# Prompt attention of a streaming encoder step: the next tile's keys are turned at the second head, its queries at the fifth

## What is computed

```python
qa, ka, va, qb, kb, vb, qi, ki, wi = _mixer_inputs(yp, pos_p, mix_norm[l], w_in[l])
# group A (x = 0): each chunk of 64 queries sees its own chunk and the 8 before it
sc = einsum('bcqhd,bckhd->bchqk', chunked(q), k_band) * (d ** -0.5)
sc = where(valid, sc + bias, -inf)
o_a = einsum('bchqk,bckhd->bcqhd', softmax(sc), v_band)
# group B (x = 1): each query sees the 256 keys that an indexer selected
sc = einsum('bqhd,bqkhd->bqhk', q, kg) * (q.shape[-1] ** -0.5)
o_b = einsum('bqhk,bqkhd->bqhd', softmax(where(valid, sc, -inf)), vg)
yp = yp + concat([o_a, o_b], axis=-1) @ w_out[l]
```

## Time and profile before

| | |
|---|---|
| median of 3 runs | 2784.23 us (2777.97 to 2785.0) |
| the profiled execution | 2785.24 us |
| its span | 2783.6 us |
| TensorE matmul busy (PE) | 2608.2 us, 94% |
| TensorE weight loads busy (PEld) | 2332.9 us, 84% |
| VectorE (DVE) | 1355.5 us, 49% |
| ScalarE (ACT) | 986.1 us, 35% |
| GpSimd (POOL) | 512.9 us, 18% |
| mean granted TensorE clock | 0.973 |
| DMA | 294.28 MB, mean 106 GB/s |

### The profile page before, as it was taken

The page is one execution under the profiler, slowest core; times in us unless marked ns, Lnnn a source line. Parts: engine busy times, 40 slices in busy tenths (PEclk is TensorE's granted clock), DMA queues, the critical chain, the costliest instruction groups (busy, mean ns, idle before and its releaser), DMA issues. The chain is left out here.

```text
span 2783.6 us, 40367 instructions
## 1 busy us (share of the span) xinstructions
PE 2608.2 (94%) x16684; PEld 2332.9 (84%) x16684; DVE 1355.5 (49%) x2437; ACT 986.1 (35%) x1666; POOL 512.9 (18%) x368
## 2 busy tenths in 40 slices
PE   6999999999999999976998989989899999999997
PEld 6999999988878899974776766657799999998886
DVE  6523232335553698985777723323642323233544
ACT  5332323233432323133666532222433232323332
POOL 0233444100001122821000000000043334410000
PEclk9999999999999999988999989999999999999999
DMA  3122221366622121213000334542112222136553
GB/s 121 48 82 73 84 80 63 121 231 209 226 108 63 65 82 48 97 35 123 24 31 24 122 108 154 178 173 85 46 63 82 72 85 80 63 118 233 194 212 121
DMA packets 153109, 294.28 MB, mean 106 GB/s; under 512 B 14032, under 2 KB 90456, under 8 KB 152928
## 3 DMA queue, kind: packets, MB, share of 16 engines
q1 hardware_dynamic: 146688, 268.12, 28.3%
q0 software_dynamic: 6240, 23.59, 2.3%
HBM read 237.26 MB, written 61.78 MB: 107 GB/s over the span
## 5 line engine op out<-in xcount | busy, mean ns | idle before, releaser
L803 DVE TENSOR_TENSOR f_dl<-f_raw_d,f_dh 128x2048 fp32r<-128x2048 f32 x66 | 151.3, 2293 | 274.6 <-ACT f_dh L619 274.6
L619 ACT ACTIVATE f_dh<-f_raw_d 128x2048 fp32r<-128x2048 f32 x66 | 126.5, 1916 | 322.1 <-PE f_pV L151 292.2
L2082 PEld LDWEIGHTS t_po<-t_v,t_pT 128*128 128x128 f32 x1056 | 134.1, 193 | 34.7 <-DVE t_osb L1806 14.3
L569 ACT ACTIVATE f_gh<-f_pX 128x256 f32<-128x256 f32 x120 | 49.3, 411 | 319.5 <-PE f_pX L151 319.5
L1939 ACT ACTIVATE t_sc<-t_sc,t_small 128x640 f32<-128x640 f32 (+8 forms) x136 | 99.9, 735 | 162.9 <-DVE t_small L1867 128.5
L150 PE MATMUL f_pX<-f_xop,f_u_shi 128*128 128x256 f32 x504 | 149.2, 296 | 0.0
L151 PE MATMUL f_pX<-f_xop,f_u_slo 128*128 128x256 f32 x504 | 149.2, 296 | 0.0
L149 PE MATMUL f_pX<-f_xop,f_u_shi 128*128 128x256 f32 x504 | 149.2, 296 | 0.0
L149 PE MATMUL w_pw<-i_hi,r_T_hi 128*128 128x256 f32 (+1 forms) x504 | 145.2, 288 | 2.6 <-PEq L351 2.6
L150 PE MATMUL w_pw<-i_lo,r_T_hi 128*128 128x256 f32 (+1 forms) x504 | 145.5, 289 | 0.0
L151 PE MATMUL w_pw<-i_hi,r_T_lo 128*128 128x256 f32 (+1 forms) x504 | 144.8, 287 | 0.0
(11 more groups left out here) (372 smaller groups left out, 8138.3 us busy)
## 6 DMA issues: line engine op xcount, KB each, us to landing
f_raw_d<-in_ffn_w_down SPq DMA_DIRECT2D x66, 1024.0 KB, 5.0
hid<-f_gh SPq DMA_DIRECT2D x22, 1152.0 KB, 9.0
f_raw_h<-hid SPq DMA_DIRECT2D x66, 384.0 KB, 5.5
f_g_raw<-in_ffn_w_gate SPq DMA_DIRECT2D x21, 1024.0 KB, 5.3
f_u_raw<-in_ffn_w_up SPq DMA_DIRECT2D x21, 1024.0 KB, 6.4
proj<-w_stage POOLq DMA_DIRECT2D x12, 1152.0 KB, 5.6
i_raw<-in_w_in SPq DMA_DIRECT2D x12, 1024.0 KB, 5.1
f_x<-in_x_prompt SPq DMA_DIRECT2D x16, 512.0 KB, 6.8
```

Of the source, the lines that this page charges most:

```text
L569: act.activation(dst, by_tile(pX[:, c, 0:N[c]]), ACT.Copy).then_inc(s_copy, 1)
L619: act.activation(d_hi[slot(q)][:], raw_d[slot(q)][:], ACT.Copy).then_inc(s_dhi, 1)
L803: dve.tensor_tensor(d_lo[slot(q)][:], raw_d[slot(q)][:], d_hi[slot(q)][:].bitcast(F32), ALU.subtract)
L2082: last = pe.matmul(po[:, h * HD:(h + 1) * HD], pT[:, g % 2, j * P:(j + 1) * P], v[x][:, k0 + j, h * HD:(h + 1) * HD], start=j == 0, stop=j ...
```

## The change

The step **prep** becomes two, **keys** and **queries**. The queries of tile n + 1 stay at h = 4, ahead of the turn. The keys move to h = 1 of tile n, behind score g + 2 and ahead of value g - 1. The list `order`, which says in which order `pm` is filled, follows: keys of n + 1, output of n - 1, queries of n + 1, where it was output, keys, queries. On TensorE the wait for the loaded rows goes with the keys; on ScalarE the copy to `kT` stands behind the exponential of head h = 3. Tile 0 keeps keys and queries one behind the other. No instruction is added or removed, and the loads' waits are unchanged.

```diff
--- before.py
+++ after.py
@@ -1515,14 +1515,16 @@
 
     heads = [(x, t, h) for x in range(2) for t in range(NP) for h in range(H)]
     tiles = [(x, t) for x in range(2) for t in range(NP)]
-    plan = [("prep", 0, 0), ("score", 0), ("score", 1)]
+    plan = [("keys", 0, 0), ("queries", 0, 0), ("score", 0), ("score", 1)]
     for g, (x, t, h) in enumerate(heads):
         n = tiles.index((x, t))
         if h == 4 and n + 1 < len(tiles):
-            plan.append(("prep",) + tiles[n + 1])
+            plan.append(("queries",) + tiles[n + 1])
         plan.append(("turn", g))
         if g + 2 < len(heads):
             plan.append(("score", g + 2))
+        if h == 1 and n + 1 < len(tiles):
+            plan.append(("keys",) + tiles[n + 1])
         if g >= 1:
             plan.append(("value", g - 1))
         if h == 2 and n >= 1:
@@ -1662,8 +1664,8 @@
             lo_n[key] = nlo
         order = []
         for e in plan:
-            if e[0] == "prep":
-                order += [(("k",) + e[1:], 0), (("q",) + e[1:], 0)]
+            if e[0] in ("keys", "queries"):
+                order += [((e[0][0],) + e[1:], 0)]
             elif e[0] == "out":
                 order += [(("o",) + e[1:], 1)]
         order += [((("sk", "sq")[j], x), 0) for x in range(2) for j in range(2)]
@@ -1942,11 +1944,13 @@
         def _(act):
             act.wait_ge(s_zero, 1)
             for e in plan:
-                if e[0] == "prep":
+                if e[0] == "keys":
+                    x, t = e[1:]
+                    act.wait_ge(s_mf, misc[("k", x, t)] + 1)
+                    act.activation(kT[x][:, :, t * P:(t + 1) * P], pm[:].rearrange("p (f c) -> p f c", c=P), ACT.Copy).then_inc(s_ma, 1)
+                elif e[0] == "queries":
                     x, t = e[1:]
                     n = x * NP + t
-                    act.wait_ge(s_mf, misc[("k", x, t)] + 1)
-                    act.activation(kT[x][:, :, t * P:(t + 1) * P], pm[:].rearrange("p (f c) -> p f c", c=P), ACT.Copy).then_inc(s_ma, 1)
                     act.wait_ge(s_mf, misc[("q", x, t)] + 1)
                     if n >= 2:
                         act.wait_ge(s_s, (n - 1) * H)
@@ -2033,11 +2037,13 @@
         @block.tensor
         def _(pe):
             for e in plan:
-                if e[0] == "prep":
+                if e[0] == "keys":
+                    x, t = e[1:]
+                    pe.wait_ge(s_row, 32 * (x * NP + t + 1))
+                    pe_rows(pe, ("k", x, t), rows[:, 0, :])
+                elif e[0] == "queries":
                     x, t = e[1:]
                     n = x * NP + t
-                    pe.wait_ge(s_row, 32 * (n + 1))
-                    pe_rows(pe, ("k", x, t), rows[:, 0, :])
                     pe_rows(pe, ("q", x, t), rows[:, 1, :])
                     if n == 0:
                         pe.wait_ge(s_bias, 16)
```

## The result

The changed kernel took 2754.56 us (median of 4 runs, 2752.39 to 2757.85), beside 2784.61 us for the kernel before; the ratio is 0.9898, with a 95% interval of 0.988 to 0.9917. Later comparisons add runs. The kernel before took 2781.3 us in the median of 32 runs (2776.98 to 2787.7), the changed one 2754.6 in the median of 8 (2750.47 to 2760.82): 26.7 us.

A forecast was written before the change was run, and what follows sets the result against it. TensorE was taken to bound the prompt attention's long tiles. 25.9 us going, less 1.4 and 2.0 coming back, saved 22.5 from 2785.24: 2762.7, or 2761.7 from the median; forecast 2762.5, range 2757 to 2773.

The forecast's parts named there:

- The base of the sum: Whole kernel: the profiled execution before the change, 2785.24 us, from which the saving was subtracted.
- What bounds, and the stall: Prompt attention: TensorE bounds long tiles; its wait for copied keys, 16.7 us in 15 waits, is removable.
- What goes, 25.9: Between keys and queries, 15 preparations: 19.3 us of stall and 6.6 of key transposes leave.
- What comes back, 1.4: Second head: key transposes mostly fit the hole before the first head's value; 1.4 us return.
- Tile 0's 0.9: Tile 0's second head: the 0.44 us of key transposes cost about 0.9 at 1.2 GHz.
- the 0.7 of the next paragraph: Tile 0: the extra 0.58 us key copy on a nearly full ScalarE loses 0.7 us.
- ScalarE's side, 2.0: Tiles 0, 1, 5, 8 and 9: the moved key copy and later ScalarE work give back 2.0 us.
- Rival (a): Tile 0 and 1459 to 1472: TensorE's low clock goes too, returning 1 to 3 us; chance 0.08.
- (b): Prompt attention: ScalarE becomes the bound, saving only 10.8 us, 2774.4; chance 0.14 with mixtures.
- (c): Bank pm: the output waits as the queries did, saving 4.4 us, about 2780.8; chance 0.06 with late loads.
- (d): Tiles 0 to 3: TensorE's clock stays at 1.2 GHz, making the kernel slower, 2798; chance 0.04.
- Loads that come late: Keys wanted after five heads, tightest in tile 1: 1.1 us at the maximum landing; shared chance 0.06.

The follow-up runs named there:

- e2: Changed kernel with the keys turned behind the first head's value at the second head, not ahead of it: 2760.14 us.
- e3: Changed kernel with the keys turned at the fourth head instead of the second, one head ahead of the queries: 2780.57 us.
- e1: The kernel before, unedited, run and profiled once more: 2781.17 us.
- e5: Changed kernel with the keys ahead of the fifth head's turn and the queries behind the score that follows it: 2761.1 us.
- e9: The changed kernel, unedited, run again: ratio 0.9915 to the kernel before.
- e4: Changed kernel with one extra ScalarE copy of the turned keys ahead of the copy to kT: 2761.4 us.
- e6: Changed kernel with the queries turned at the sixth head instead of the fifth: 2758.0 us.
- e7: Changed kernel with the third head's turn issued ahead of the first head's value: 2755.22 us.
- e8: Changed kernel with queries at the sixth head and the third head's turn ahead of the first head's value: 2752.46 us.
- e11: Changed kernel with three extra chained ScalarE copies of the turned keys ahead of the copy to kT: 2770.97 us.

## Why the prediction was right and wrong

Two steps of the prediction failed, and either alone would have left the time inside the range. The base of the sum, 2785.24 us (the range allowed for 1.0 less), lies 3.9 above the median of 32 runs; what was put down as coming back, 1.4 + 2.0 = 3.4 us, measured 1.9 (1.4 in tile 0, 0.4, 0.6 and 0.2 in the spacings of tiles 5, 7 and 13, less 0.8 of small gains in the others), and the clock in tile 9, put at nothing in the sum, gave 1.3. (2781.3 less the 22.5 forecast is 2758.8, and 2784.23 less the 26.7 measured is 2757.5: both lie in the range.)

**What bounds, and the stall: right.** TensorE's wait for t_kT was a pure loss. With it out, a five-block tile is shorter by 1.69 us (1.6 forecast), heads stay 2.69 to 2.70 apart, and nothing behind the stretch changed its length.

**What goes, 25.9: right.** For the 14 preparations between the first and the last output the gaps from keys to queries sum to 24.0 us; the gain there was 24.8, of which 1.3 are the clock in tile 9. All 15 gaps sum to 25.9.

**What comes back, 1.4: too high.** The holes took the key transposes in all middle tiles (e2: 0.42 to 0.44 each when they can't). Tile 14 lost 0.26 of the 0.44 put down for it. Tile 0's 0.9 can be had only together with the 0.7 of the next paragraph. From its first turn to the first output it took 14.59 and 15.23 us in two profiles of before (14.59 in e3 as well), 14.11 and 14.12 in two of after. Its gap was 1.92, so 1.4 us were lost against the profiled run and 0.8 against e1, where the clock was down for longer; forecast were 1.6.

**ScalarE's side, 2.0: too high.** Two of its terms measured as forecast: tile 5 gained 1.84 of its 2.23 (0.3 forecast as lost, 0.39 lost), and tile 8's output got a wait, 0.49 marked, which cost 0.60 in the spacing (1.05 of 1.65). Tile 5's loss stands where it was forecast, at the sixth head:

```profile
1376.52 0.74 PE L2028 MATMUL t_pt<-r_ident,t_sc 128*128 128x128 f32 x5 [0.25 <-ACT t_pT L1977]
```

But tiles 1 and 8 gained 0.22 and 0.15 more than their gaps, where I had put losses of 0.2 each. In tiles 1 and 9 the loss is there, a new wait of a value for t_pT of 0.23 each; what covers it is the wait for T_lo at the fifth head, which fell from 1.02 to 0.57 in tile 1, from 1.29 to 1.00 in tile 8 and from 0.77 to 0.60 in tile 9. I had counted on that for tile 1 alone. And I left out a gain: queries that follow a value directly take 0.44 to the next turn, not the 0.49 they took behind a stall, 0.05 in each tile (24.66 to 22.97 is 1.69, and the gap was 1.65).

**Rival (a), 0.08: it came.** The low stretch of the clock in tile 9 is in all three profiles that have the spacings of the kernel before (before, e1, e3) and in neither of after. Before (two windows), then after at the same place in the program, over a longer window:

```profile
1469.00:1472.00 3.00, 2.39 (x10) 2.22 (x11) 0.01 (x1) 1.81 (x5) 0.00 (x0) 0.62 0.10 23
1472.00:1475.00 3.00, 3.00 (x20) 2.68 (x19) 2.34 (x9) 1.85 (x7) 0.00 (x0) 0.81 0.46 157
```

```profile
1440.00:1459.00 19.00, 16.52 (x108) 13.51 (x109) 15.73 (x48) 13.07 (x41) 0.00 (x0) 1.00 0.10 29
```

Tile 9 gained 2.83 us where the gap was 1.55: 1.3 us of clock, the term that (a) priced at 1.2. I should have given it more than a chance of 0.08. The likely cause is idle time of TensorE, which the change removes. The Trainium skill's rule ("TensorE: Matmul & The Clock Gate", part 1), weighed in the prediction, pointed that way; in this tile the trace agrees, with 0.62 before and 1.00 after. That the stall behind the keys is the cause is not shown: e2 and e5, where it is gone or small, have low stretches in tile 12, e2 also in tile 8. Between tile 0 and the last output six of the twelve profiles have none (after, e9, e4, e6, e7, e8, all with the keys in the hole at the second head) and six have at least one; e11, with the keys there and ScalarE held up, is one of these. But tile 12's wait of 1.52 us for t_osb is the same in before, at 1.00 behind it, as in e2 and e5. No run isolates idle time as the cause.

**The base: wrong, and the other half of the miss.** I counted from 2785.24 us. Only 3 of 32 runs of before took longer; their median is 2781.3. The three runs that I had spread over 7.0 us and their mean was 2782.4, so the range should have had more than 1.0 us for the base. So the miss of 7.9 us is 3.9 from the base and 4.2 from the saving (26.7 by medians over all runs, 25.3 by the mean of two profiles each, for the 22.5 forecast), less 0.2 of rounding. Of the 4.2, 1.5 are losses that were put too high (1.9 instead of 3.4), 1.3 are tile 9's clock, and 1.4, the difference between 26.7 and 25.3, are not seen in the stretch of any profile. The division goes by all runs; in the first comparison, of four runs each, the kernel before had 2784.61 and the saving was 30.0.

**The other rivals.** (b) is out by e4; of the waits for t_pT that would have shown it, long tiles have only tile 5's. (c) lives in one tile: the output of tile 8. (d) didn't come: 1297 to 1344 was at 1.00 throughout. Loads that come late were not seen either; no wait for t_rows is left but the first.

## What to carry to other kernels

When one engine walks a plan together with others, a step has a place in each engine's order, and what a wait costs is set by the two places together: moving the producer's part past work in which the copying engine has no share (e3) changes nothing. Fill a hole of the bounding engine with work that it must do anyway, and look for the hole with the named wait: here it paid 0.44 us a tile for the keys and 2.8 us more for a turn (e7). Count from the middle of many runs of the old kernel, not from the one that was profiled.

## What the runs showed of the hardware that I had not expected

The same code ahead of the stretch ended anywhere between 1262.4 and 1271.1 us in twelve profiles, with granted clocks of 0.98 and 1.00 in the same 100 us window. TensorE's clock fell in short tiles without any long stop: in e1 to 0.51 in a stretch of 3 us that follows one with TensorE busy 1.31 of 3.00 us at 1.00.

```profile
1460.40:1463.40 3.00, 1.31 (x10) 0.94 (x10) 1.70 (x5) 1.86 (x6) 0.00 (x0) 1.00 0.02 5
1463.40:1466.40 3.00, 3.00 (x14) 2.82 (x15) 0.71 (x5) 1.65 (x4) 0.00 (x0) 0.51 0.33 84
```

And the prompt attention itself repeats to 0.02 us a tile where the clock stays at 1.00, so that edits worth 0.4 us can be read from spacings in a profile while the whole time spreads by 10.
